# Top-k threshold search: six tiles compared on VectorE, their counts summed on ScalarE

## What is computed

```python
h = jnp.einsum('bld,de->ble', x, w_in)                   # input projection
...
score = jnp.where(admissible[None], score, -jnp.inf)
top_val, top_idx = lax.top_k(score, k_sel)               # 256 keys of up to 2048
...
xbc, conv_new = causal_dwconv(xbc, conv_prev, conv_w, conv_b)   # ends in SiLU
```

## Time and profile before

| what | us |
|---|---|
| median of 3 runs (lowest, highest) | 2790.87 (2769.73, 2792.38) |
| the profiled execution, its span | 2787.39, 2785.5 |
| mean granted TensorE clock, of full speed | 0.959 |
| busy over the span: TensorE, VectorE, ScalarE, GpSimd | 2536.7, 2135.8, 1028.7, 783.1 |
| accumulating compares of the search (L863), 256 + 224 with a candidate | 370.0 + 315.7 |
| high-part casts on ScalarE (L779), 80 | 80.2 |
| low-part subtractions on GpSimd (L830), 80 | 201.3 |

### The profile page before, as it was taken

The page is one execution under the profiler, slowest core; times in us unless marked ns, Lnnn a source line. Parts: engine busy times, 40 slices in busy tenths (PEclk is TensorE's granted clock), DMA queues, the critical chain, the costliest instruction groups (busy, mean ns, idle before and its releaser), DMA issues. The chain is left out here.

```text
span 2785.5 us, 39144 instructions
## 1 busy us (share of the span) xinstructions
PE 2536.7 (91%) x14786; PEld 2201.8 (79%) x14787; DVE 2135.8 (77%) x3443; ACT 1028.7 (37%) x1889; POOL 783.1 (28%) x796
## 2 busy tenths in 40 slices
PE   7998969999998999989879867899999988799997
PEld 5887769999998888989856635777777777688886
DVE  3799799999999999989789935677766667344442
ACT  3678521212221112214423324555555556222221
POOL 1010323323333233445469903322111021000000
PEclk8999989999999999999989987999999999899998
DMA  7330062222325333348535334212110046322220
GB/s 247 103 96 4 1 222 94 82 88 94 92 77 204 95 95 95 129 134 257 171 106 174 137 107 126 78 57 57 44 37 29 20 139 234 121 91 91 91 91 23
DMA packets 187478, 294.68 MB, mean 106 GB/s; under 512 B 29451, under 2 KB 131734, under 8 KB 185751
## 3 DMA queue, kind: packets, MB, share of 16 engines
q1 hardware_dynamic: 164489, 220.30, 25.2%
q0 software_dynamic: 22800, 71.88, 7.2%
HBM read 181.92 MB, written 110.20 MB: 105 GB/s over the span
## 5 line engine op out<-in xcount | busy, mean ns | idle before, releaser
L863 DVE TENSOR_SCALAR_CACHE_REDUCE project_junk<-all_S,project_cand 128x528 bf16<-128x528 f32 (+7 forms) x256 | 370.0, 1445 | 1.1
L766 PE MATMUL PS<-project_wh,project_xh 128*128 128x256 f32 x1224 | 347.7, 284 | 0.0
L766 PE MATMUL PS<-project_xh,project_wh 128*128 128x384 f32 (+1 forms) x880 | 316.6, 360 | 34.1 <-DMA project_xl<-x_parts 34.1
L766 PE MATMUL PS<-project_wl,project_xh 128*128 128x256 f32 x1224 | 346.7, 283 | 0.0
L766 PE MATMUL PS<-project_wh,project_xl 128*128 128x256 f32 x1224 | 346.6, 283 | 0.0
L2211 DVE TENSOR_TENSOR attend_ptl<-PS,attend_pth 128x512 fp32r<-128x512 f32 x272 | 185.3, 688 | 173.2 <-ACT attend_pth L2073 172.7
L766 PE MATMUL PS<-project_xh,project_wl 128*128 128x384 f32 (+1 forms) x880 | 315.7, 359 | 0.0
L863 DVE TENSOR_SCALAR_CACHE_REDUCE project_tie<-all_S,project_cand 128x384 bf16<-128x384 f32 (+6 forms) x224 | 315.7, 1409 | 0.0
L766 PE MATMUL PS<-project_xl,project_wh 128*128 128x384 f32 (+1 forms) x880 | 315.6, 359 | 0.0
L766 PEld LDWEIGHTS PS<-project_wl,project_xh 128*128 128x128 f32 x1224 | 235.1, 192 | 0.0
L766 PEld LDWEIGHTS PS<-project_wh,project_xh 128*128 128x128 f32 x1224 | 235.1, 192 | 0.0
(11 more groups left out here) (328 smaller groups left out, 5730.2 us busy)
## 6 DMA issues: line engine op xcount, KB each, us to landing
project_raw<-in_w_in SPq DMA_DIRECT2D x80, 512.0 KB, 4.3
featT<-project_st POOLq DMA_DIRECT2D x66, 192.0 KB, 2.1
all_S<-featT SPq DMA_DIRECT2D x12, 1024.0 KB, 5.6
featT<-project_st POOLq DMA_DIRECT2D x44, 256.0 KB, 2.3
x_parts<-index_s_x POOLq DMA_DIRECT2D x10, 1024.0 KB, 7.2
gate_s<-project_st POOLq DMA_DIRECT2D x68, 128.0 KB, 2.1
gate_a<-project_st POOLq DMA_DIRECT2D x68, 128.0 KB, 2.2
ssd_x<-x_tok SPq DMA_DIRECT2D x17, 512.0 KB, 4.8
```

The lines of the kernel that those rows point to most:

```text
L766: last = nc.tensor.matmul(PS[:, r % 8, 0:w], lhsT, rhs, start=(k == 0 and j == 0), stop=(k == KT - 1 and j == 2))
L863: v.tensor_scalar((junk, tie)[j % 2][:, 0:L], tile_scores(j), th, None, op, ALU.add, accum_out=into[:, j:j + 1]).then_inc(counted, 1)
```

## The change

In each pass, VectorE compares the six widest tiles (2048 down to 1408 keys, `SUM`) without counting, into `junk` and `tie` in turn. ScalarE adds each result up with a Copy that has an accumulator (L822 of the changed kernel), which overwrites the compared row. The other nine tiles (`DIRECT`) are counted on VectorE as before, into a third row `spare` (it lies where `rank` lies, which is used only later). Compare `i` waits for sum `i - 2` (two rows), and the small operations wait for all sums of the pass. Where the sums stand among ScalarE's evictions is set by a plan: `at` adds up TensorE's time by output, and sum `i` of pass `p` is put in front of the first output that ends, by the plan, at or behind `20 p + 2.4 i + 3` us (`PASS_US`).

The count for SiLUs and transposes now starts with the ninth block from the end, with `silu_at` 7, 11, 15, ... 52 instead of 4, 8, 11, ... 45. SP stores all masks and begins to load tokens at the eighth block from the end.

```diff
+        rank_at = m.end
         rank = m("rank", [P, SEQ], mybir.dt.int16)
+        spare = b.map("spare", rank_at)("spare", [P, SEQ], BF16)
...
-        LATE = 5 * (HALF[1][1] - HALF[1][0])
-        silu_at = [int(4.5 + 3.7 * f) for f in range(NF2)]
+        LATE = (len(cols) - NF) * (HALF[1][1] - HALF[1][0])
+        silu_at = [int(7 + 4.1 * f) for f in range(NF2)]
...
-                if hf and n >= len(cols) - 5:
+                if hf and n >= NF:
...
+        SUM = [SEL.index(t) for t in range(TILES - 1, 9, -1)]
+        WIDE, SLIM = [SEL.index(t) for t in (9, 8, 7, 6)], [SEL.index(t) for t in (5, 4, 3, 2, ST)]
+        DIRECT = [SLIM[i // 2] if i % 2 == 0 else WIDE[i // 2] for i in range(len(WIDE) + len(SLIM))]
...
+        PASSES, PASS_US = 33, 20.0
+        sums_before, at, todo = {}, 0.0, 0
+        for r, (_, _, kind, _, _, w) in enumerate(outs):
+            at += {"f": w * 24 * 0.00045, "t": 2.9, "x": 0.45}[kind]
+            n = 0
+            while (todo < PASSES * len(SUM)
+                   and todo // len(SUM) * PASS_US + todo % len(SUM) * 2.4 + 3.0 <= at):
+                todo, n = todo + 1, n + 1
+            sums_before[r] = n
...
-                    if blk == NBLK - 5:
-                        store_masks(LOWS, mask_st[0])
...
-                    if blk == NBLK - 5:
+                    if blk == NBLK - 8:
+                        store_masks(LOWS, mask_st[0])
                         store_masks([t for t in SEL if t not in LOWS], mask_st[1])
...
-                    if blk > NBLK - 5:
-                        for f in (2 * (blk - NBLK + 4), 2 * (blk - NBLK + 4) + 1):
+                    if NBLK - 7 <= blk < NBLK - 7 + (NF2 - 2) // 2:
+                        for f in (2 * (blk - NBLK + 7), 2 * (blk - NBLK + 7) + 1):
                             sp.wait_ge(conv, CONV_OPS * (f + 1))
                             load_tokens(f + 2)
-                for f in range(8, NF2 - 2):
-                    sp.wait_ge(conv, CONV_OPS * (f + 1))
-                    load_tokens(f + 2)
...
+                        for q in range(q, q + sums_before[r]):
+                            j, rows = SUM[q % len(SUM)], (junk, tie)[q % 2]
+                            L, into = keys_of(SEL[j]), above if q // len(SUM) == PASSES - 1 else count
+                            act.wait_ge(compared, q + 1)
+                            ac(rows[:, 0:L], rows[:, 0:L], ACT.Copy, accum_out=into[:, j:j + 1]).then_inc(summed, 1)
+                        q += 1 if sums_before[r] else 0
                         act.wait_ge(proj, r + 1)
...
+                    def compare(i):
+                        q, j = n * len(SUM) + i, SUM[i]
+                        wait(dve, summed, q - 1)
+                        v.tensor_scalar((junk, tie)[q % 2][:, 0:keys_of(SEL[j])], tile_scores(j), bound(j), None, op
+                                        ).then_inc(compared, 1)
+
+                    def direct(i):
+                        q, j = n * len(DIRECT) + i, DIRECT[i]
                         L = keys_of(SEL[j])
-                        th = against if isinstance(against, float) else against[:, j:j + 1]
-                        v.tensor_scalar((junk, tie)[j % 2][:, 0:L], tile_scores(j), th, None, op, ALU.add,
+                        o = keys_of(9) if j in SLIM else 0
+                        wait(dve, counted, q - 1)
+                        v.tensor_scalar(spare[:, o:o + L], tile_scores(j), bound(j), None, op, ALU.add,
                                         accum_out=into[:, j:j + 1]).then_inc(counted, 1)
+                    for i in range(len(DIRECT)):
+                        if i < len(SUM):
+                            compare(i)
+                        direct(i)
+                    dve.wait_ge(counted, (n + 1) * len(DIRECT))
+                    dve.wait_ge(summed, (n + 1) * len(SUM))
```

More of the change, by code:

```diff
@@ L621, in stage_project @@
         step, counted, sel = sem("step"), sem("counted"), sem("sel")
+        compared, summed = sem("compared"), sem("summed")
         SEL_STEPS = 2 + 5 * NSEL
@@ L668, in stage_project @@
         NBLK = len(used)
+        SUM = [SEL.index(t) for t in range(TILES - 1, 9, -1)]
+        WIDE, SLIM = [SEL.index(t) for t in (9, 8, 7, 6)], [SEL.index(t) for t in (5, 4, 3, 2, ST)]
+        DIRECT = [SLIM[i // 2] if i % 2 == 0 else WIDE[i // 2] for i in range(len(WIDE) + len(SLIM))]
+        assert len(SUM) + len(DIRECT) == NSEL and keys_of(9) + keys_of(5) <= SEQ
+        PASSES, PASS_US = 33, 20.0
[7 more added lines that the diff above has]
+            sums_before[r] = n
+        assert todo == PASSES * len(SUM)
         silu_last = [f for f in range(NF2) if f not in silu_before.values()]
@@ L796, in _ @@
                 high(1)
-                r = 0
+                r, q = 0, 0
                 for blk in range(NBLK):
@@ L854, in tile_scores, with counts, bound @@
                     return S[:, SOFF[SEL[j]]:SOFF[SEL[j]] + keys_of(SEL[j])]
[L856 to L860, removed]
+                def counts(n, against, op, into):
+                    def bound(j):
+                        return against if isinstance(against, float) else against[:, j:j + 1]
+                    def compare(i):
[5 more added lines that the diff above has]
+                        q, j = n * len(DIRECT) + i, DIRECT[i]
                         L = keys_of(SEL[j])
-                        th = against if isinstance(against, float) else against[:, j:j + 1]
-                        v.tensor_scalar((junk, tie)[j % 2][:, 0:L], tile_scores(j), th, None, op, ALU.add,
+                        o = keys_of(9) if j in SLIM else 0
+                        wait(dve, counted, q - 1)
+                        v.tensor_scalar(spare[:, o:o + L], tile_scores(j), bound(j), None, op, ALU.add,
                                         accum_out=into[:, j:j + 1]).then_inc(counted, 1)
+                    for i in range(len(DIRECT)):
[4 more added lines that the diff above has]
+                    dve.wait_ge(summed, (n + 1) * len(SUM))
                 dt, NTL = b.dt, TILES + 1
@@ L896, in _ @@
                 counts(0, 0.0, ALU.is_ge, count)
-                dve.wait_ge(counted, NSEL)
                 v.tensor_tensor(hit[:, :], count[:, :], want[:, :], ALU.is_ge).then_inc(step, 1)
@@ L912, in _ @@
                     dve.wait_ge(step, 5 + 3 * i + 1)
-                    counts((i + 1) * NSEL, candf, ALU.is_ge, count)
-                    dve.wait_ge(counted, (i + 2) * NSEL)
+                    counts(i + 1, candf, ALU.is_ge, count)
                     v.tensor_tensor(hit[:, :], count[:, :], want[:, :], ALU.is_ge).then_inc(step, 1)
@@ L921, in _ @@
                 dve.wait_ge(sel, 1)
-                counts(32 * NSEL, candf, ALU.is_gt, above)
-                dve.wait_ge(counted, 33 * NSEL)
+                counts(32, candf, ALU.is_gt, above)
                 v.tensor_tensor(room[:, :], want[:, :], above[:, :], ALU.subtract).then_inc(sel, 1)
```

## The result

| | before | after |
|---|---|---|
| median of 9 runs each (lowest, highest), us | 2788.39 (2769.14, 2794.29) | 2811.02 (2808.66, 2812.31) |
| span of the profiled execution | 2785.5 | 2807.6 |
| search ends | 1103.5 | 1041.5 |
| TensorE's first wait for a SiLU | 8.1 | 24.0 |
| lost at the end of the projection stage | 19.4 | 37.0 |

The changed kernel is slower: 22.6 us by the medians (0.8%), 22.1 by the spans of one profiled execution each, and 1% by the ratio (1.0101, 95% interval 1.0078 to 1.0124). The runs of the kernel before spread over 25 us, so these measures differ. "Lost" is worked out as in the prediction: the end of the last matmul, less the start of the token blocks (the first eviction's start less 2.88), less 223.6 for 72 outputs and 8 groups of transposes. After, from ScalarE's first eviction of a token block and TensorE's last matmul: 1394.44 - 1133.86 - 223.6 = 37.0.

A forecast was written before the change was run, and what follows sets the result against it. TensorE's own work bounds the projection stage. From SiLU 0's end at 1190.2, 200.8 us more gives 1391.0 (+15.6); a shorter stage end (-1.2) makes +14.4, taken as 2803 us, range 2767 to 2835.

The forecast's parts named there:

- The bound of 19.4 us: End of the projection stage: at most 19.4 us lost by TensorE, 0.7% of the run, can come back.
- Holds: Search on VectorE: GpSimd's subtraction pairs block compares and small operations, 1.8 us a pass (bounds 0 and 3.4).
- The sums: Search on ScalarE: six sums take 9.5 to 11.6 us a pass and fit among its evictions and casts.
- The plan sets the pace, search end 1041: Search: VectorE, at 17.9 us a pass, waits at a pass's end for the last sum; search end 1041, against 1103.5.
- Ranking 130 us: Ranking and masks after the search: 105 us unheld plus 25 for six GpSimd pairs, until 1171.
- 29 us of idle time: TensorE at the first x transposes: arrives at 1161.2, waits for SiLU 0 until 1190.2, where before it waited 8.1.
- Some 4 us of lower clock and 2 us of small losses: TensorE after SiLU 0: these losses come on top of 62 outputs (178.6 us) and 8 groups (16.2).
- No further stall follows: TensorE behind the first stall: convolutions come every 10.2 us and it needs one per 13.8, so no more stalls.
- Tail 4.7 us: Stage end: from TensorE's last matmul to SP's first next-stage load, 4.7 us instead of 5.9.
- just in time: Rival: ranking's holds mostly vanish, search ends at 1037, SiLU 0 is done as TensorE arrives; 2769 us, chance 0.16.
- Behind the plan: Rival: mutual waits and double holds make search passes 21.5 us, search end 1070.7; 2831 us, chance 0.20.
- Not cheaper: Rival: unaccumulated compares run at the old rate, passes stay 22.5 us, search end 1104; 2865 us, chance 0.03.

The follow-up runs named there:

- the run with the old schedule: The changed kernel's new search, with SiLUs, transposes, mask stores and token loads back at the places of the kernel before: 2770.73 us, ratio 0.9956.
- the one with the old search: The kernel before with only the new schedule of SiLUs, transposes, mask stores and token loads: 2855.13 us, ratio 1.0242.
- the best version: The changed kernel with the schedule of before and eight staging buffers of 256 columns instead of four of 512: 2767.92 us, ratio 0.9929.
- Narrow staging: The changed kernel with its four staging buffers of 512 columns cut into eight of 256: 2801.36 us, ratio 1.0061.

## Why the prediction was right, and where it was off

The predicted time was 2803, the measured 2811.02, inside the range, in the forecast's own (2793 to 2815) and at the slow edge of the step "within 1%" (0.8% by the medians, 1.0% by the ratio). The forecast's mechanism holds: the run with the old schedule and the one with the old search show that the moved deadline costs and the search gains. The bound of 19.4 us holds as well, within 1.5 us: the best version loses nothing in the stage and is 20.9 us below the kernel before.

- *The compares*: 1.26 us predicted, 1.29 measured for 2048 keys. *Holds*: 1.8 us a pass predicted. Measured: the six means exceed their unheld like (1.29 us for 2048 keys, 1.15 for 1792, 0.95 for 1408) by 1.2 us together, the small operations' means (0.51 + 0.25 + 0.17 us, unheld 0.17 each) by 0.4: 1.6 us. A compare of 1792 keys took 1.15 us or, in eight of 33 rows, 1.9 to 3.3. The Trainium skill's rule ("SBUF — State Buffer", "Who interferes with whom"), that a VectorE operation in a 2-port mode waits out a whole GpSimd instruction, agrees with these rows as far as one subtraction of 2.4 us; the longest compare, 5.10 us where 3.4 had been put as the most, is more than one subtraction.
- *The sums*: 9.5 to 11.6 us a pass predicted; six means of 1.37 to 1.91 us make 9.8, with six reads 11.0. ScalarE waited only 18.2 us for compares in the whole search.
- *The plan sets the pace, search end 1041*: 1041.5. VectorE waited for sums 3.2 us a pass (48.2 + 43.4 + 14.1 us), but only 14.1 of them at the end of a pass, where the prediction had it wait; the rest fell on compares that needed a summed row. With passes planned at 18 us the search ended 65 us sooner.
- *Ranking 130 us*: 126.4. Only five pairs met it, since ScalarE stood at SiLU 0 from 1154 on and cast no weights for a sixth. The prediction took this into account for the first convolution, but not for ranking.
- *29 us of idle time*: 24.0. SiLU 0 was done 3.7 us earlier than put, and TensorE came to it 1.5 us later.
- *"Some 4 us of lower clock and 2 us of small losses" behind the first wait*: this term was mis-sized. From SiLU 0's end to the last matmul it took 208.0 us against 194.8 of work, so 13.2 instead of 6. The excess is in the small losses: 8.3 us of waits (1.75, 1.63 and 4.36 on SiLUs, 0.58 on an eviction) instead of 2; the other 4.9, the lower clock among them, are near the 4. "No further stall follows" looked at convolutions alone (10.2 us against 13.8); the SiLUs stand in ScalarE's order behind evictions that wait for stores. Narrow staging took 10.8 of the stage's loss away.
- *Tail 4.7 us*: 7.2. SP's load came 6.0 us behind the end of the last store's issue (1395.70), where 3 had been put between TensorE's end and the landing.

The two mis-sized terms (+7.2, +2.5), the early SiLU (-3.7) and 1.7 us more in the later stages make the 7.7 us between the forecast change of 14.4 and the 22.1 of the spans. That the early SiLU hid a part of the two was luck. Of the rivals, *just in time* missed: the holds in ranking stayed. *Behind the plan* missed: the pass was 20.6 us long on average, its waits for sums included. *Not cheaper* missed: 1.29 us.

## What to carry to other kernels

When work off the critical path gets faster, don't move its consumer's place in a fixed order by more than it gained: here 62 us were won, the deadline moved by 83, and at the old place TensorE would not have waited for the first SiLU at all. An engine that works in order passes on every wait in its queue, so look for what stands ahead of the instruction that others wait for (here evictions at full staging buffers), and cut buffers to the size of what goes through them. Moving one gate shows the next, so read which transfers queue behind the one that is moved past. And where two engines hold each other up, work that comes earlier can lengthen the very chain that it was to shorten.

## What the runs showed of the hardware

- The length of a search with the same code changed by 19 us between two kernels that differ only behind it, the kernel before and the one with the new schedule. VectorE and GpSimd fall into step. In this stretch GpSimd's pairs of subtractions start 24.96 us apart in both kernels, and a pass that meets no pair takes 21.04 us. In the kernel before, the small operations of the second pass (402.20) meet a pair (402.27), wait it out, and so meet the next one too: eleven passes in a row take 24.96 to 25.29 us. In the other kernel they come at 402.65, end before the pair of 403.98, and the two fall into step only at the eighth pass, for six passes. Five held passes less at 3.9 us are the 19 us. GpSimd's pair and the operation that it holds, before:

```profile
427.23 4.74 POOL L830 TENSOR_TENSOR project_wl<-project_raw,project_wh 128x1024 fp32r<-128x1024 f32 x2 [0.20 <-ACT project_wh L779]
```

```profile
427.48 2.17 DVE L915 TENSOR_TENSOR project_hit<-project_count,project_want 128x15 int32<-128x15 f32 x1
429.69 2.31 DVE L917 SCALAR_TENSOR_TENSOR project_key<-project_hit,project_key 128x15 int32<-128x15 int32 x1
```

  What moved the pair by 1.7 us between the kernels is not shown.

- GpSimd's DMA issues took longer at times during the new search: the same stores, first in the kernel before, then after (shortest, median and longest in ns):

```profile
L842 POOL DMA_DIRECT2D featT<-project_st x93: 542/542/572, 369.9 to 1040.8; - x93
```

```profile
L863 POOL DMA_DIRECT2D featT<-project_st x92: 540/542/1507, 371.2 to 1036.9; - x92
```

The median stayed, the longest went from 0.57 to 1.51 us. The Trainium skill, in "SBUF — State Buffer", "Who interferes with whom", says that GpSimd's making of descriptors starves while a VectorE operation holds the shared ports, which agrees with these rows. The long issues go with the search and not with the schedule: the longest is 1.55 us with the new search and the old schedule, 0.57 with the old search and the new schedule. That the unaccumulated compares cause it, and not the sums, was not tried by itself. It cost TensorE nothing that shows in the search, as the old schedule with the new search tells.
